# A two-block transformer on one core: U of the expert stage 26 steps ahead of V, one compare for both one-hots

## What is computed

```python
def _peer(h, w_pq, sub_keys, peer_u, peer_v):
    qp = (h @ w_pq).reshape(b, s, PEER_HEADS, 2, PEER_HALF)
    sc = jnp.einsum("bshpd,hpnd->bshpn", qp, sub_keys)
    s1, i1 = lax.top_k(sc[..., 0, :], PEER_TOPK)
    s2, i2 = lax.top_k(sc[..., 1, :], PEER_TOPK)
    cand = (s1[..., :, None] + s2[..., None, :]).reshape(b, s, PEER_HEADS, PEER_TOPK * PEER_TOPK)
    top_s, top_c = lax.top_k(cand, PEER_TOPK)
    e1 = jnp.take_along_axis(i1, top_c // PEER_TOPK, axis=-1)
    e2 = jnp.take_along_axis(i2, top_c % PEER_TOPK, axis=-1)
    expert = e1 * N_KEYS + e2
    gate = jax.nn.softmax(top_s, axis=-1)
...
        u = jnp.take(peer_u, e_c, axis=0)
        a = jnp.einsum("bcd,bchkd->bchk", h_c.astype(jnp.float32), u.astype(jnp.float32))
        w = g_c * jax.nn.gelu(a)
        vv = jnp.take(peer_v, e_c, axis=0)
        return jnp.einsum("bchk,bchkd->bcd", w, vv.astype(jnp.float32))
...

x = x + gate2 * _peer(h2, w_pq, sub_keys, peer_u, peer_v)
```

## Time and profile before

| | |
|---|---|
| median of 3 runs | 2832.74 us |
| the profiled execution, its own time | 2838.91 us |
| its span, first to last instruction | 2837.1 us |
| mean granted TensorE clock | 0.955 |
| TensorE matmul busy, share of the span | 2532.2 us, 89% |
| VectorE | 1786.5 us, 63% |
| ScalarE | 955.8 us, 34% |
| GpSimd | 355.3 us, 13% |

### The profile page before, as it was taken

One profiled execution on the slowest core, in us unless ns is written; L12 is line 12 of the kernel. 1 busy time (PEld: TensorE's weight loads), 2 busy tenths in 40 slices (PEclk: granted clock), 3 DMA queues, 4 the chain that ended last, 5 costly groups with the idle time before them and its releaser, 6 DMA issues.

```text
span 2837.1 us, 37492 instructions
## 1 busy us (share of the span) xinstructions
PE 2532.2 (89%) x13633; PEld 2153.2 (76%) x13633; DVE 1786.5 (63%) x3871; ACT 955.8 (34%) x1639; POOL 355.3 (13%) x326
## 2 busy tenths in 40 slices
PE   8999888999989969989256669999999999999998
PEld 6777776777779747854156668898989898899986
DVE  5535646553244455458887657877777777776675
ACT  3334412222224446311134444333333333333332
POOL 1001100110000000100000001232222222222220
PEclk9999989999999989999678899999999999999999
DMA  4110005662222110030003345787777777777764
GB/s 172 61 45 1 1 33 183 228 216 88 79 86 75 60 45 1 1 126 1 8 23 141 149 170 190 261 292 261 268 261 270 265 269 267 266 272 277 244 224 141
DMA packets 107908, 427.20 MB, mean 151 GB/s; under 512 B 11328, under 2 KB 11584, under 8 KB 97104
## 3 DMA queue, kind: packets, MB, share of 16 engines
q1 hardware_dynamic: 62624, 262.17, 26.2%
q0 software_dynamic: 44064, 160.98, 16.3%
q10 hardware_dynamic: 1040, 1.67, 0.2%
HBM read 397.51 MB, written 27.26 MB: 150 GB/s over the span
## 4 chain that ended last, share of the span: by engine, by line
PE 73%; DVE 14%; issue 4%; ACT 4%; DMA 2%; DVEq 2%; ACTq 1%; SPq 1%; POOLq 0%
PE ps L2023 16%; PE ps L2007 15%; PE ps L1808 9%; PE ps L1762 7%; PE ps L1678 5%; PE ps L1830 4%; PE ps L1996 3%; PE ps L2056 3%; PE ps L1743 2%; DMA gd<-big 1%; PE ps L1948 1%; PE ps L1715 1%; PE ps L1929 1%; ACT r L639 1%; PE ps L1730 1%
## 5 line engine op out<-in xcount | busy, mean ns | idle before, releaser
L2007 PE MATMUL ps<-hd_hi,uT_hi 128*128 128x384 f32 x1024 | 349.4, 341 | 0.7 <-ACT r L864 0.7
L2007 PE MATMUL ps<-hd_hi,uT_lo 128*128 128x384 f32 x1024 | 347.4, 339 | 0.0
L2007 PE MATMUL ps<-hd_lo,uT_hi 128*128 128x384 f32 x1024 | 347.3, 339 | 0.0
L1488 DVE TENSOR_TENSOR uT_lo<-ps,uT_hi 128x512 fp32r<-128x512 f32 x256 | 176.7, 690 | 255.0 <-ACT uT_hi L845 254.8
L2023 PE MATMUL ps<-v_hi,ew_hi 128*128 128x512 f32 x768 | 320.4, 417 | 3.9 <-DVE v_lo L1493 2.1
L2023 PE MATMUL ps<-v_hi,ew_lo 128*128 128x512 f32 x768 | 303.1, 395 | 0.0
L2023 PE MATMUL ps<-v_lo,ew_hi 128*128 128x512 f32 x768 | 300.9, 392 | 0.0
L537 POOL DMA_INDIRECT big<-peer_u,r x128 | 136.0, 1062 | 861.6 <-DVE r L1563 524.8
L845 ACT ACTIVATE uT_hi<-ps 128x512 fp32r<-128x512 f32 x256 | 152.9, 597 | 266.3 <-PE ps L1996 266.3
L864 ACT ACTIVATE r<-ps,zero 128x384 f32<-128x384 f32 x128 | 74.3, 581 | 472.0 <-PE ps L2007 467.7
L1996 PE MATMUL ps<-const,r 128*128 128x128 f32 x1024 | 155.3, 274 | 52.5 <-DVE uT_lo L1488 32.9
(11 more groups left out here) (332 smaller groups left out, 5335.2 us busy)
## 6 DMA issues: line engine op xcount, KB each, us to landing
big<-wst SPq DMA_DIRECT2D x70, 1024.0 KB, 4.8
r<-peer_u SPq DMA_DIRECT2D x128, 512.0 KB, 7.2
r<-peer_v SPq DMA_DIRECT2D x128, 512.0 KB, 5.2
r<-wada POOLq DMA_DIRECT2D x48, 512.0 KB, 4.7
gd<-big SPq DMA_DIRECT2D x12, 2048.0 KB, 15.1
big<-gd SPq DMA_DIRECT2D x32, 768.0 KB, 9.4
x<-x_in SPq DMA_DIRECT2D x4, 512.0 KB, 6.7
big<-peer_u,r POOLq DMA_INDIRECT x128, 6.4
```

The lines of the kernel that those rows point to most:

```text
L1488: v.tensor_tensor(uT_lo[:, s % 2], ps[:, 1, :].rearrange("p (k n) -> p k n", k=KD // 2), uT_hi[:, s % 2].bitcast(F32), ALU.subtract).then_ ...
L2007: mm = pe.matmul(ps[:, 0, 0:DN], w[:, k, :], h[:, KD // 2 * half + k, :], start=(half == 0 and k == 0 and i == 0), stop=(half == 1 and k = ...
```

## The change

- `AHEAD` is 26. The ring's first ten places lie in the tile `x`, the others in the scores' memory; so the residual is stored to a DRAM tensor `xd` before the router and read back in loop step 106 (`xback`).
- U steps 0 to 7 lie behind the last eight pairs of the router, step 8 behind the ranks of tile 0, steps 9 and 10 round its first chunks; 11 to 14, 15 to 18 and 19 to 25 follow tiles 0, 1 and 2 (`BEFORE`). None is left between the chunks.
- One compare of 2048 columns makes both one-hots of a chunk. ScalarE multiplies the second with the gate: eight copies of 128 columns, in place, with a per-partition scale.
- ScalarE issues the four stores of a staged tile, in its own stream.
- Picks are split: `tile_ranks` (ranks and compares) and `tile_picks` (gates, one reduction over 4096 columns). GpSimd does the product in between, but for one of two sides of tile 0. Ranks and picks of tiles 1 and 2 lie between the chunks of tile 0.
- Rows of tile 3 are spread over steps 4 to 102; `finish3` stays at step 112.

```diff
-AHEAD = 16
+AHEAD = 26
+INX = 10
+BEFORE = (11, 15, 19, 26)
...
-FIRST_ROW, LAST_ROW = 4, 112
+FIRST_ROW, LAST_ROW = 4, NE - AHEAD
...
-        act_ring = cut(r2, 0, AHEAD, DN)
+        x_flat = x.rearrange("p t d -> p (t d)")
+        act_ring = ([x_flat[:, DN * s:DN * s + DN] for s in range(INX)]
+                    + [r2[:, DN * (AHEAD - 1 - s):DN * (AHEAD - s)] for s in range(INX, AHEAD)])
...
+            sp.wait_ge(out_add, 8 * T)
+            for t in range(T):
+                sp.dma_start(xd[t], x[:, t, :]).then_inc(x_out, 16)
...
+                if i == LAST_ROW + 4:
+                    sp.wait_ge(u_row, SLOTS)
+                    sp.wait_ge(v_row, SLOTS)
+                    sp.wait_ge(x_out, 16 * T)
+                    for t in range(T):
+                        sp.dma_start(xback[t], xd[t]).then_inc(x_back, 16)
...
+            def slot_keys(t):
+                pool.wait_ge(ranks_ready, t + 1)
+                for a in range(2 if t else 1):
+                    hk = hot[:, a].rearrange("p (h k) r -> p h k r", h=PH)
+                    mk = pool.tensor_tensor(hk, hk, each_pick(a), ALU.mult)
+                mk.then_inc(hot_ready, 1)
...
+            act.wait_ge(x_out, 16 * T)
+            u_high(0)
+            for j in range(9):
+                hidden_evac(j)
+                if j in (5, 6, 7):
+                    gate_exps(j - 5)
+            def gated(t, c):
+                n = t * NCH + c
+                act.wait_ge(keys_equal, n + 1)
+                for k in range(CHUNK):
+                    at = 2 * P + CHUNK * c + k
+                    mk = act.activation(one[n % 2][1][:, k, :], one[n % 2][1][:, k, :], ACT.Copy, scale=slotT[t][:, at:at + 1])
+                mk.then_inc(one_ready, 1)
...
             for t in range(DT):
                 stage_free(act, t)
                 for c in range(NCH):
+                    if c + 1 < NCH:
+                        gated(t, c + 1)
...
+                act.wait_ge(g_ev, 2 * NCH * (t + 1))
+                for q in range(4):
+                    act.dma_start(gd[t][:, 4096 * q:4096 * q + 4096], stage[:, 32 * q:32 * q + 32, :].rearrange("p e t -> p (e t)")
+                                  ).then_inc(g_out[q], 16)
+                if t + 1 < DT:
+                    gated(t + 1, 0)
+                for j in range(BEFORE[t], BEFORE[t + 1]):
+                    if j < AHEAD - 1:
+                        hidden_evac(j)
...
                     pair_tops(t, h).then_inc(top_done, 1)
+                    u = DT * h + t - 16
+                    if u == 0:
+                        u_low(0)
+                    if u >= 0:
+                        hidden_low([u])
+            tile_ranks(0)
+            hidden_low([8])
...
-                    v.tensor_tensor(one1[:, n % 2], each(keys, CHUNK), over(slotT[t][:, CHUNK * c:CHUNK * c + CHUNK], NKEYS),
-                                    ALU.is_equal).then_inc(one1_ready, 1)
-                    for k in range(CHUNK):
-                        at = CHUNK * c + k
-                        mk = v.tensor_scalar(one2[:, n % 2, k, :], keys, slotT[t][:, P + at:P + at + 1],
-                                             slotT[t][:, 2 * P + at:2 * P + at + 1], ALU.is_equal, ALU.mult)
-                    mk.then_inc(one2_ready, 1)
...
+                    e12 = slotT[t][:, 0:2 * P].rearrange("p (a s) -> p a s", a=2)[:, :, CHUNK * c:CHUNK * c + CHUNK]
+                    v.tensor_tensor(one_pair[n % 2], each(keys, 2 * CHUNK).rearrange("p (a s) n -> p a s n", a=2), over(e12, NKEYS),
+                                    ALU.is_equal).then_inc(keys_equal, 1)
+                    if t == 0 and c in (3, 9):
+                        tile_ranks(c // 6 + 1)
+                    if t == 0 and c in (6, 12):
+                        tile_picks(c // 6)
+                    if t and c == 1:
+                        hidden_low(range(BEFORE[t - 1], BEFORE[t]))
+            hidden_low(range(BEFORE[DT - 1], AHEAD))
+            v.wait_ge(g_out[1], 16 * DT)
```

More of the change, by code:

```diff
@@ L246, in build @@
         stage = cut(big, 0, NKEYS, P)
-        one1 = cut(r1, 0, 2, CHUNK, P)
-        one2 = cut(r1, 2 * CHUNK * P, 2, CHUNK, P)
+        one = [[cut(r1, CHUNK * P * (2 * b + a), CHUNK, P) for a in range(2)] for b in range(2)]
+        one_pair = [cut(r1, 2 * CHUNK * P * b, 2, CHUNK, P) for b in range(2)]
         slotT = [gates[:, 0, 0:384], gates[:, 0, 384:768], r1[:, 10240:10624]]
[L250 to L255, removed]
+        xback = [cut(big, 8192 + D * i, D) for i in range(T)]
+        hot = cut(r2, 0, 2, SLOTS, TOPK)
+        rank_bits = cut(r2, 14368, 2, SLOTS).bitcast(U32)
+        ranks = cut(r2, 14624, 2, SLOTS)
+        wrap = cut(big, NKEYS * P, SLOTS)
+        topf = cut(r1, 11104, 2, SLOTS)
+        picks = [v.rearrange("p (a s) -> p a s", a=2) for v in (gates[:, 0, 768:1024], r1[:, 10848:11104], rowsb[:, 0:256])]
         gring = cut(big, 0, 2, DT, GB * P)
@@ L1509, in w_low, with hidden_low @@
                                 ALU.subtract).then_inc(ew_lo_done, 1)
+            def hidden_low(steps):
+                for j in steps:
+                    u_low(2 * j + 1)
+                    u_low(2 * j + 2)
             for h in range(PH):
@@ L1638, in _ @@
                         picks3(h)
-                if i == LAST_ROW:
+                if i == LAST_ROW + 10:
                     finish3()
@@ L2041, in _ @@
             u_transposes(0)
-            experts_in(0)
-            for t in range(DT):
-                slot_transposes(t)
-            experts_in(1)
+            for j in range(9):
+                experts_in(j)
+            slot_transposes(0)
+            for j in range(9, BEFORE[0]):
+                experts_in(j)
             for t in range(DT):
@@ L2055, in _ @@
                         for k in range(4):
-                            mm = pe.matmul(ps[:, 4 + u % 4, P * k:P * k + P], one1[:, n % 2, 4 * half + k, :],
-                                           one2[:, n % 2, 4 * half + k, :], start=True, stop=True)
+                            mm = pe.matmul(ps[:, 4 + u % 4, P * k:P * k + P], one[n % 2][0][:, 4 * half + k, :],
+                                           one[n % 2][1][:, 4 * half + k, :], start=True, stop=True)
                         mm.then_inc(g_acc, 1)
-                    if c % 4 == 3:
-                        experts_in(2 + 4 * t + c // 4)
-            for j in range(2 + 4 * DT, AHEAD):
-                experts_in(j)
+                    if t == 0 and c in (8, 14):
+                        slot_transposes(c // 7)
+                for j in range(BEFORE[t], BEFORE[t + 1]):
+                    experts_in(j)
             for i in range(NE):
```

130 lines of the change are left out of this document (64 added, 66 removed).

## The result

The changed kernel takes 2871.48 us in the median of 4 runs (2865.26 to 2876.58), the kernel before 2832.06 beside it: 1.0138 times as long, 95% interval 1.0116 to 1.0160. It is slower, as forecast, but by 39 us where I had 11, and outside the range (2814 to 2860).

What follows compares the result with a forecast made beforehand. TensorE was taken to bound the expert loop, waits the stretch before it: loop start 53 us later, minus 51 for ten steps, plus 5 denser rows, 2 read-back, 2 clock, is +11 us: median 2843, range 2814 to 2860.

Steps and rivals of the forecast that it cites:

- Router: Top-k pairs: VectorE waits 14.3 us at the first U residual; first step 5.3 us, seven more 2.74 each.
- Picks of tile 0: Before the gates: GpSimd's 4.5 us product hides under U step 8 and costs nothing; gates start on ScalarE at 1455.
- rival 3: Picks of tiles 1 and 2: GpSimd's products hold VectorE's compares, 4 us more a tile, 2855 in all; chance 0.15.
- Tile 0: Gates of tile 0: 16 chunks of 4.10 us on ScalarE plus 1.2, 1 and 13, together 80.8 us.
- my 13: Gates of tile 0: VectorE's ranks and picks of tiles 1 and 2 stall ScalarE 3.7 and 2.6 us, two of each.
- Tiles 1 and 2: Their gates: ScalarE paces chunks at 4.10 us, with copies 0.295 us apart; 64.4 us for each tile.
- rival 1: Gates: ScalarE's scaled copies only 0.22 us apart, a chunk 3.50 us, 2814 in all, faster; chance 0.15.
- Seams and end: Between tiles: store issue 3.3, gating 2.5, four U steps 21.7, gelu 0.8, so 28.3 us; last seven steps 40.1.
- The ten steps: Expert loop: ten U steps leave it, each worth 9.28 - 4.16 = 5.12 us, 51 us gained.
- Denser rows: Expert loop: tile 3's rows in 98 steps instead of 108 may add 0 to 10 us, taken as 5.
- Reading `x` back: V-only loop steps: reading 2 MB of residual back can hold a V load, 0 to 5 us, taken as 2.
- rival 2: Seams hide more than counted, at most 13 + 5 + 2 us; half gone gives 2833, no change; chance 0.21.

Runs made afterwards that it cites:

- run 6: Changed kernel, the second residual of each U step in the router standing half a pair later: 2857.31 us, 1.0090 times the kernel before.
- run 10: Changed kernel, products and one-hots on VectorE, stores issued by GpSimd, the 26 steps laid anew over router, picks, chunks and seams: 2806.78 us, 0.9911.
- run 7: Changed kernel without GpSimd's five products of ranks and keys, done by nobody (picks and gates hold other numbers): 2861.22 us, 1.0111 times the kernel before.
- run 8: Changed kernel, GpSimd writing ones in place of its product (picks and gates hold other numbers): 2859.51 us, 1.0094 times the kernel before.
- Run 2: Changed kernel, both one-hots made by VectorE as before the change, ScalarE's scaled copies gone: 2841.87 us, 1.0043 times the kernel before.
- run 4: Kernel before the change, only the rows of tile 3 spread over steps 4 to 102 instead of 4 to 112: 2837.88 us, 1.0028.

## Why the prediction was wrong in size

Its path to the loop was, on the marks used here, 402.4 us (96.1 to the gates, 80.8 for tile 0, twice 28.3 and 64.4, 40.1 at the end); measured 427.9. Its loop, with the cold clock, was 1128.1 - 51 + 9 = 1086; measured 1092.8.

- **Router**: 14.31 us of waiting, forecast 14.3; a step 2.73 in the rows, forecast 2.74. The first step took 1.5 us longer than the 5.3 I gave it, and single rows of the seven pairs behind it 0.5 more. Right; run 6 shows that much of what the steps cost there need not be, and run 10 that the wait need not.
- **Picks of tile 0: the failed step.** "GpSimd's product costs nothing here: 4.5 us from 1428 ends under step 8." It was over before step 8's residuals (1429.7 against 1431.9), but it had begun beside the second compare and held it for 4.4 us. Runs 7 and 8 show the cause. I had the mechanism as rival 3, yet saw it only for tiles 1 and 2.
- **Tile 0: the same step.** Forecast 80.8, measured 95.0; 84.8 without the product. My rival priced the lock at 4 us a tile and 12 in all; the rows have VectorE held 4.4 + 2 x 8.5 = 21 us, of which 14.6 reach the path in the profiles of run 7 and 10.3 in its median. The other 4.0 us of tile 0 stand mostly in run 7's own rows: ScalarE still waits 16.4 us for VectorE's compares there, 3.4 more than my 13, 1.2 of it ahead of the first block and most of the rest at the picks (3.7 and 4.0 us, forecast 2.6 each). The Trainium skill, SBUF — State Buffer, SBUF: two separate sides, states an exclusive lock for the whole instruction between a vector operation with two SBUF inputs and a GpSimd operation that reads SBUF; 9.05 against 4.66 us, and the writes of run 8 that hold nothing, agree with both halves of it. I gave this 0.15 because no row of before had both engines at work; nothing spoke against it either.
- **Tiles 1 and 2**: forecast 64.4 each, measured 64.3 and 63.8. Right, and with it rival 1 falls: 0.29 us a copy, not 0.22. The price operand by operand, from three exps of the same shape, was the best term of the sum. Run 2 shows these copies to be the largest cost that a single edit took away (29.6 us).
- **Seams and end**: forecast 28.3, 28.3 and 40.1, measured 30.1, 29.1 and 42.0. The issues took 3.8, 3.6 and 2.2 us, 3.3 forecast; the store was covered, as said.
- **The ten steps: the second failed step.** "9.28 - 4.16 = 5.12 us." The 9.28 holds what the rows of tile 3 add. Those rows all stay, so what leaves the loop is a step without them: 9.05 - 4.16 = 4.89 us, 2.3 us less gain for ten. Between run 4 and the changed kernel, with the same rows in the same steps, the part from step 102 on shrank by 46.7 (10 x 4.89 = 48.9).
- **Denser rows**: 5 forecast, 6.3 by the two profiles and 7.6 by the medians. Right in kind and near in size. The start of the loop cost 5.2 where I had 2 for the clock. Reading `x` back, 2 in the sum: behind step 102 ScalarE waits 1.4 us for rows of V, and VectorE's longest wait for a high copy of V is 1.6 us, against 0.4 in run 4; I put it at about 1, an estimate from these waits.

Set right, the path to the loop had 25.5 us more than my sum (14.6 of it the lock, 3.7 seams, end and tiles 1 and 2 together, 2.0 the router, 5.2 the rest of tile 0 and of the picks) and the loop 6.7, less the 4.8 by which the earlier stages came out shorter (chance: the last copy of scores lies between 1348.0 and 1358.9 us in the profiles of these runs, with the same stages ahead of it): 27.4, against 26.6 between 2850 and 2876.6. The sign was right, and the largest cost was the forecast one, the pace of ScalarE; "the seams hide more" (rival 2) went the other way.

## What to carry to other kernels

Before work is given to an idle engine, look at what the busy one does at that moment: here a product that takes 2.3 us on VectorE took 4.5 on GpSimd and stopped VectorE's compares all that time, so that the help gained nothing: with the products on VectorE the kernel took 2870.9 us, with GpSimd's help 2871.5. When steps are moved out of a loop, price them by the iterations that will be gone, not by the mean of all: what shares the mean but stays is no gain. And work moved ahead is worth what the place hides: beside the router's pairs a U step cost 1.2 us, among chunks 3.0, alone 5.7, in the loop 4.9; the same 26 steps made the kernel 39 us slower or, laid elsewhere and with ScalarE relieved, 24 us faster.

## What the runs showed of the hardware

- A GpSimd product that reads SBUF and a VectorE compare of two SBUF tensors exclude each other for whole instructions: 9.05 us for 4.66 of compares beside a product of 4.48, and 15.36 for three beside two. A GpSimd write of the same 2048 columns (3.55 us for two) beside the same compares costs them nothing. The residuals of U, which read one operand from PSUM, had no case beside a product.
- A GpSimd product of 2048 columns takes 4.48 us, VectorE's 2.28.
- ScalarE's in-place copy of 128 columns with a per-partition scale: 394 ns, 0.29 us from start to start.
- Four stores cost ScalarE 2.2 to 3.8 us of issue, GpSimd 2.17 in this row of its timeline with the stores there:

```profile
1550.20 2.17 POOL L558 DMA_DIRECT2D gd<-big  x4 [27.68 <-ACT big L950]
```
